# A two-block transformer on one core: another order of work in the mixing stages, and rank roots kept as four columns

## The reference

```python
# block one, mixing (8 query heads, 2 key groups, head size 64)
kc = _rope(_compress(k_cmp), ...)        # gelu(blocks @ w1) @ w2: 15 compressed keys
vc = _compress(v_cmp)
p_cmp = softmax(q @ kc)                  # compressed attention
# selected (slc), windowed (win) and sliding (swa) attention follow; then
merged = sigmoid(ga) * (o_a @ w_branch_a) + sigmoid(gb) * (o_b @ w_branch_b)
h = h + merged @ w_out

# block two, mixing
q  = rmsnorm(cq, g_q) @ w_uq             # rank 768 -> 8 heads x 96, rope on 32 of 96
kv = rmsnorm(ckv, g_kv) @ w_ukv          # rank 256 -> keys and values of 8 heads
o_a = mla_attention(...)                 # dense, 8 heads
o_b = dsa_attention(...)                 # sparse: index scores, top 64, 4 heads
o_c = silu(rg) * head_groupnorm(retention(...))
x = x + concat(o_a, o_b, o_c) @ w_out
```

## Time and profile before

| what | value |
|---|---|
| median of 3 runs | 1364.92 us (1363.53 to 1365.43) |
| profiled execution | 1365.18 us, of it 1363.3 us from the first to the last instruction |
| mean granted TensorE clock | 0.973 of 2.4 GHz |
| TensorE busy | 1316.5 us |
| VectorE busy | 823.7 us |
| ScalarE busy | 628.6 us |
| GpSimd busy | 95.3 us |

### The profile page before, as it was taken

How to read it: one execution, slowest core, us unless ns; L and a number is a source line. 1 busy time by engine, 2 the same in 40 slices (tenths; PEclk the granted TensorE clock), 3 DMA queues, 4 the chain that set the end, 5 groups by cost and what they waited for, 6 DMA issues and landing times.

```text
span 1363.3 us, 21639 instructions
## 1 busy us (share of the span) xinstructions
PE 1316.5 (97%) x8900; PEld 1196.4 (88%) x8900; DVE 823.7 (60%) x947; ACT 628.6 (46%) x838; POOL 95.3 (7%) x73
## 2 busy tenths in 40 slices
PE   6999999999989999999999999999999999999997
PEld 4999998888979999998889789999988878899996
DVE  2665547656556565555689766555557876655554
ACT  4344445466533543334743445444464344544443
POOL 0000001200000000000542100000004230000000
PEclk7999999989989999999989899999999999999999
DMA  7555556443214565556523235555644231465551
GB/s 234 187 190 186 186 165 172 141 151 94 93 63 145 179 217 185 185 185 178 166 87 127 93 93 175 189 190 186 178 155 141 84 124 57 149 212 186 187 189 54
DMA packets 173347, 209.93 MB, mean 154 GB/s; under 512 B 24168, under 2 KB 149728, under 8 KB 173152
## 3 DMA queue, kind: packets, MB, share of 16 engines
q1 hardware_dynamic: 172976, 208.78, 48.6%
q10 hardware_dynamic: 304, 0.20, 0.1%
HBM read 207.92 MB, written 1.05 MB: 153 GB/s over the span
## 4 chain that ended last, share of the span: by engine, by line
PE 87%; DVE 5%; ACT 4%; issue 2%; POOL 1%; DMA 1%; SPq 0%; ACTq 0%; DVEq 0%; POOLq 0%
PE bank L1726 69%; PE bank L2156 4%; PE bank L2018 3%; PE bank L2039 2%; ACT w_hi L920 2%; DVE w_lo L1254 2%; PE bank L1795 2%; PE bank L1961 1%; PE bank L2025 1%; PE bank L1783 1%; POOL scr L847 1%; DMA raw<-in_ffn_gate_dram 1%; PE bank L2073 1%; ACT scr L951 1%; PE bank L2012 1%
## 5 line engine op out<-in xcount | busy, mean ns | idle before, releaser
L1254 DVE TENSOR_TENSOR w_lo<-raw,w_hi 128x2048 fp32r<-128x2048 f32 (+1 forms) x198 | 449.0, 2269 | 296.6 <-ACT w_hi L920 296.0
L1726 PE MATMUL bank<-n_hi,w_hi 128*128 128x256 f32 (+2 forms) x1696 | 488.8, 288 | 13.4 <-DVE w_lo L1254 11.4
L1726 PE MATMUL bank<-n_lo,w_hi 128*128 128x256 f32 (+2 forms) x1696 | 484.4, 286 | 0.0
L1726 PE MATMUL bank<-n_hi,w_lo 128*128 128x256 f32 (+2 forms) x1696 | 484.3, 286 | 0.0
L920 ACT ACTIVATE w_hi<-raw 128x2048 fp32r<-128x2048 f32 (+1 forms) x198 | 369.5, 1872 | 236.0 <-PE bank L1726 215.7
L1726 PEld LDWEIGHTS bank<-n_hi,w_hi 128*128 128x128 f32 (+2 forms) x1696 | 328.2, 194 | 20.2 <-DVE w_lo L1254 12.2
L1726 PEld LDWEIGHTS bank<-n_lo,w_hi 128*128 128x128 f32 (+2 forms) x1696 | 328.2, 194 | 2.3 <-issue 0.5
L1726 PEld LDWEIGHTS bank<-n_hi,w_lo 128*128 128x128 f32 (+2 forms) x1696 | 328.0, 193 | 0.0
L1726 PE MATMUL bank<-w_hi,hid_hi 128*128 128x512 f32 (+1 forms) x472 | 182.8, 387 | 1.8 <-DVE hid_lo L1321 1.5
L1726 PE MATMUL bank<-w_lo,hid_hi 128*128 128x512 f32 (+1 forms) x472 | 181.6, 385 | 0.0
L1726 PE MATMUL bank<-w_hi,hid_lo 128*128 128x512 f32 (+1 forms) x472 | 181.1, 384 | 0.0
(11 more groups left out here) (250 smaller groups left out, 1554.1 us busy)
## 6 DMA issues: line engine op xcount, KB each, us to landing
raw<-in_w_ff_dram SPq DMA_DIRECT2D x64, 1024.0 KB, 5.2
raw<-in_w_in_dram SPq DMA_DIRECT2D x31, 1024.0 KB, 5.3
raw<-in_ffn_gate_dram SPq DMA_DIRECT2D x22, 1024.0 KB, 5.3
raw<-in_ffn_up_dram SPq DMA_DIRECT2D x22, 1024.0 KB, 5.4
raw<-in_ffn_down_dram SPq DMA_DIRECT2D x22, 1024.0 KB, 4.9
raw<-in_w_out_dram SPq DMA_DIRECT2D x12, 1024.0 KB, 5.0
raw<-in_w_uq_dram SPq DMA_DIRECT2D x8, 576.0 KB, 4.1
raw<-in_w_in_dram SPq DMA_DIRECT2D x12, 256.0 KB, 4.1
```

What stands on the lines that cost most here:

```text
L1254: V.tensor_tensor(w_lo[:, s % SPLIT, 0:n], raw[:, s % RING, 0:n], w_hi[:, s % SPLIT, 0:n].bitcast(f32), ALU.subtract).then_inc(lo_ready, 1)
L1726: mm = MM(out, stat(k, a), mov(k, b), start=(first and k == 0 and n == 0), stop=(last and k == K - 1 and n == 2), skip_group_check=True)
```

## The change

Three things change.

In block one the compression of the keys moves in front of the first scores and the rest of the fill list moves up by one place: the compressed scores come behind `gate 3` instead of `gate 5`, their weighted sums behind `gate 5` and `gate 6`, and `gate 7` behind the whole attention. The compressed scores become one matmul for both key groups: the rope writes the two groups to separate row halves of `kcR`, the other halves stay zero, and 4 matmuls over 128 rows and 32 columns take the place of 8 over 64 rows and 16 columns.

In block two the roots of the ranks are taken on four columns instead of a 128 x 512 tile: the sums come out of 4 matmuls of one column (`rank`, now after `proj rk`, with GpSimd's sum in a step `rsum` at the old place), the root is taken there (`rank`, `rinv`), and a step `spread` behind `proj rq` brings it to all rows, from four diagonal matrices in `diag_r`. `rtok` goes.

Also in block two, `krope` and `ukv` move into the sparse attention, the ropes `uq2` and `uq3` between its weighted sums, and `rety` into the dense attention, behind its last scores. The group norm works in `rvt` instead of `o_tmp`.

```diff
-          ("xpe", "k"), ..., ("rope", 0, "nq1"), ("rope", 0, "sq1")]
-    fill = [("cmp1", "k"), ("cmp1", "v")] + [("gate", n) for n in range(8)]
+          ("xpe", "k"), ..., ("rope", 0, "nq1"), ("rope", 0, "sq1"), ("cmp1", "k")]
+    fill = [("cmp1", "v")] + [("gate", n) for n in range(7)]
     after = {("cmp1", "v"): [("cmpt", "k")], ("gate", 0): [("cmp2", "k"), ("cmpt", "v")],
-             ("gate", 1): [("cmp2", "v"), ("rope", 0, "kc")], ("gate", 5): [("cs", 0), ("cs", 1)],
-             ("gate", 6): [("ct", 0), ("o", 0, "cmp", 0)], ("gate", 7): [("ct", 1), ("o", 0, "cmp", 1)]}
+             ("gate", 1): [("cmp2", "v"), ("rope", 0, "kc")], ("gate", 3): [("cs", 0), ("cs", 1)],
+             ("gate", 5): [("ct", 0), ("o", 0, "cmp", 0)], ("gate", 6): [("ct", 1), ("o", 0, "cmp", 1)]}
...
-    S += [("ot", "a", 0), ("ot", "a", 1), ("ot", "b", 0), ("ot", "b", 1), ("branch",)]
+    S += [("gate", 7), ("ot", "a", 0), ("ot", "a", 1), ("ot", "b", 0), ("ot", "b", 1), ("branch",)]
...
-              ("proj", l, "ckv"), ("idx", l, 0), ("proj", l, "aq"), ("idx", l, 1), ("rank", l), ("idx", l, 2),
-              ("proj", l, "rk"), ("rope", l, "aq"), ("idx", l, 3), ("idx", l, 4), ("proj", l, "rq"), ("rope", l, "rk"),
+              ("proj", l, "ckv"), ("rsum", l), ("idx", l, 0), ("proj", l, "aq"), ("idx", l, 1), ("idx", l, 2),
+              ("proj", l, "rk"), ("rank", l), ("rope", l, "aq"), ("idx", l, 3), ("rinv", l), ("idx", l, 4), ("proj", l, "rq"),
+              ("spread", l), ("rope", l, "rk"),
...
-              ("proj", l, "rg"), ("rtok", -l), ("rope", l, "kr"), ("topk", l, 1, 0, 4), ("uq", l, 0),
+              ("proj", l, "rg"), ("rope", l, "kr"), ("topk", l, 1, 0, 4), ("uq", l, 0),
...
-        S += attention(l, [("dsa", 0), ("dsa", 1)], [("retn", l), ("uq", l, 3)], {}, 1)
-        S += [("rety", l), ("rope", l, "uq2"), ("rope", l, "uq3")]
-        S += [("krope", l), ("ukv", l)]
-        S += attention(l, [("mla", 0), ("mla", 1)], [], {}, 2)
+        S += [("s", l, "dsa", 0, 0), ("s", l, "dsa", 1, 0), ("s", l, "dsa", 1, 1), ("retn", l), ("uq", l, 3), ("krope", l),
+              ("t", l, "dsa", 0, 0), ("ukv", l), ("t", l, "dsa", 1, 0), ("pv", l, "dsa", 0, 0), ("o", l, "dsa", 0),
+              ("t", l, "dsa", 1, 1), ("rope", l, "uq2"), ("pv", l, "dsa", 1, 0), ("rope", l, "uq3"), ("pv", l, "dsa", 1, 1),
+              ("o", l, "dsa", 1)]
+        dense = attention(l, [("mla", 0), ("mla", 1)], [], {}, 2)
+        late = dense.index(("t", l, "mla", 1, 1))
+        S += dense[:late] + [("rety", l)] + dense[late:]
...
# GpSimd, krope
-                    pool.wait_ge(turnc_ready, RO[(l, "uq3")] + 1)
-                    pool.wait_ge(pv_done, ON[(l, "dsa", 1)][1])
+                    pool.wait_ge(*free_count(("s", l, "dsa", 1, 1)))
...
# ScalarE
+                elif kind == "rinv":
+                    act.wait_ge(rank_inv, st[1])
+                    for i in range(2):
+                        for t in range(NT):
+                            last = nc.scalar.activation(diag_r[:, i, t, :], con("ident"), ACT.Copy, scale=rrank[:, i, t:t + 1])
+                    last.then_inc(rank_diag, 1)
+                elif kind == "spread":
                     pb = await_bank(act, st)
-                    nc.scalar.activation(rtok[:, 2, :], pb[:, 0:T:P], ACT.Copy).then_inc(freed(st), 1)
+                    nc.scalar.activation(rstd[:, 1:3, :], halves(pb[:, :]), ACT.Copy).then_inc(r_ready, 1)
...
# VectorE, rank and rinv
+                    r = rtok[:, 0:1, :].to_broadcast([P, 2, NT])
+                    V.tensor_tensor(rrank[:, :, :], pb[:, 0:4].rearrange("p (i t) -> p i t", i=2), r, ALU.mult).then_inc(freed(st), 1)
...
+                elif kind == "rinv":
                     dve.wait_ge(rank_std, st[1])
-                    link(V.reciprocal(part, part))
-                    V.tensor_tensor(part, part, r2(), ALU.mult).then_inc(r_ready, 1)
+                    link(V.reciprocal(rrank[:, :, :], rrank[:, :, :]))
+                    V.tensor_tensor(rrank[:, :, :], rrank[:, :, :], rtok[:, 0:1, :].to_broadcast([P, 2, NT]), ALU.mult).then_inc(rank_inv, 1)
...
# TensorE, cs
-                    for h in range(8):
-                        if h == 4:
-                            settle(mm)
-                        r = slice(64 * (h // 4), 64 * (h // 4) + 64)
-                        mm = MM(pb[:, h * CP:h * CP + CP], nqT[r, h % 4, t * P:t * P + P], kcR[r, h // 4, :], start=False, stop=True,
-                                skip_group_check=True)
+                    by_group = pb[:, 0:P].rearrange("p (g r c) -> p r g c", g=2, r=4)
+                    for r in range(4):
+                        mm = MM(by_group[:, r], nqT[:, r, t * P:t * P + P], kcR[:, :, :], start=False, stop=True, skip_group_check=True)
...
# TensorE, rank and spread
-                    MM(pb[:, 0:T], ones[:, :], sq[:, 0, :], start=True, stop=True)
-                    MM(pb[:, T:2 * T], ones[:, :], sq[:, 6, :], start=True, stop=True).then_inc(filled(st), 1)
+                    for i in range(2):
+                        for t in range(NT):
+                            mm = MM(pb[:, 2 * i + t:2 * i + t + 1], sq[:, 6 * i, t * P:t * P + P], ones[:, 0:1], start=True, stop=True)
+                    mm.then_inc(filled(st), 1)
+                elif kind == "spread":
+                    pb = take(pe, st)
+                    pe.wait_ge(rank_diag, st[1])
+                    for i in range(2):
+                        for t in range(NT):
+                            c = (2 * i + t) * P
+                            mm = MM(pb[:, c:c + P], ones[:, :], diag_r[:, i, t, :], start=True, stop=True)
+                    mm.then_inc(filled(st), 1)
```

More of the change, by code:

```diff
@@ L381, in job @@
         def job(key, b=None, freed_by=None, of_slab=False):
-            if b is None and idle[0] and key[0] in ("rope", "rtok", "toks", "idx", "rank"):
+            if b is None and idle[0] and key[0] in ("rope", "toks", "idx", "rank", "spread"):
                 b = _small[0] % 4
@@ L879, in _ @@
                     add_up([(slice(0, 3), slice(3, 6)), (0, 1), (0, 2), (6, 7)])
+                if st[0] == "spread":
                     pool.wait_ge(r_ready, RN[st] + 1)
@@ L1499, in _ @@
                     ahead(SL[st])
+                    dve.wait_ge(r_ready, RN[("spread", st[1])] + 1)
                     for n in range(4):
@@ L1519, in _ @@
                     dve.wait_ge(turnc_ready, r + 1)
-                    V.tensor_tensor(dst, view[2], view[0], ALU.add).then_inc(rope_done, 1)
+                    if st[2] == "kc":
+                        for g in range(2):
+                            rows_ = slice(64 * g, 64 * g + 64)
+                            last = V.tensor_tensor(dst[rows_, g], view[2][rows_, g], view[0][rows_, g], ALU.add)
+                        last.then_inc(rope_done, 1)
+                    else:
+                        V.tensor_tensor(dst, view[2], view[0], ALU.add).then_inc(rope_done, 1)
                     turn_used[0] = (rope_done, r + 1)
@@ L1872, in _ @@
                         mm = nc.tensor.transpose(pb[:, t * w_:t * w_ + w_], by_feature[0:w_, t * P:t * P + P], ident[0:w_, 0:w_])
-                    mm.then_inc(filled(st), 1)
-                elif kind == "rtok":
-                    pe.wait_ge(r_ready, RN[("rank", -st[1])] + 1)
-                    pb = take(pe, st)
-                    for t in range(NT):
-                        mm = nc.tensor.transpose(pb[:, t * P:t * P + P], rstd[:, 2, t * P:t * P + P], ident)
                     mm.then_inc(filled(st), 1)
```

33 lines of the change are left out of this document (16 added, 17 removed).

## The result

| what | before | changed |
|---|---|---|
| median | 1365.18 us (1363.53 to 1365.64, 4 runs) | 1349.84 us (1347.48 to 1354.16, 4 runs) |
| profiled execution, its span | 1365.18, 1363.3 us | 1347.48, 1345.7 us |
| mean granted clock in it | 0.973 | 0.989 |

The ratio is 0.990, 95% interval 0.9879 to 0.9922: 15.3 us less at the median, 17.6 us between the two profiled spans. The four executions of the changed kernel lie further apart than those of before (6.7 us against 2.1), and the profiled one is their fastest, so what follows accounts for the 17.6 us and not for the 15.3. The forecast was 1346.0 us, in 1336 to 1356.

The account below looks back on a forecast made before the run. TensorE, busy 97% of the span, was taken as the bound; 5.4 + 8.0 + 0.9 + 2 x (4.3 + 3.5 - 2.0) = 25.9 us, less 6.8 for clock falls, gave 19.1: 1365.1 to 1346.0 us, range 1336 to 1356.

Parts of the forecast that it names:

- Part 1 and 2: Block one: compression ahead of first scores, net 5.4 us despite a new 2.1 us wait; joined compressed scores, 8.0 us.
- Part 3: Tail of block one's attention: 1.51 us wait goes, 1.93 us wait grows by 0.6; gain 0.9 us.
- Part 4: Rank roots, both layers: the wait for GpSimd's sum and its half clock go; net gain 4.3 us each.
- rival (c): Rank change trades its wait for one behind GpSimd; ending slower than before, 1365 us and up; chance 0.03.
- Part 5: Key-value slab inside the sparse attention, both layers: 6.1 us go, new waits come; net gain 3.5 us each.
- three blocked splits: Key-value slab: GpSimd's copy and both rope products each block a split, some 2 us worse per layer.
- Part 6: Group norm's end inside the dense attention, both layers: four VectorE instructions delay a copy; loss 2.0 us each.
- Four places: Block one's first weighted sum, both dense attentions, compressed scores: clock falls, even chances, 3.4 us each; -6.8 us for two.
- rival (b): Whole kernel: new waits are longer and the clock falls at all four places, 1352 to 1357 us; chance 0.23.
- (a): Whole kernel: the clock never falls again, gain 26 us or a little more, 1333 to 1339 us; chance 0.17.
- Rival (d): Whole kernel: half-clock stretches return as long as before, only waits move; gain about 0 to 6 us; chance 0.07.

Follow-up runs that it names:

- the second profile: The changed kernel run once more, unchanged, beside the kernel before: 1350.22 us (1348.07 to 1351.09), ratio 0.9892.

## Why the prediction was right, and where a step of it was wrong

The sum was 25.9 us without falls, 19.1 with two of four; 17.6 us came in the profiled execution and 15.3 at the median. The terms were further off than their sum: the key-value part gave 2.2 us less than forecast (both layers) and block one 1.2 less, while the rank roots gave 0.9 more and the clock cost 5.6 us in place of 6.8. That these nearly cancel is luck.

- **Part 1 and 2, block one.** Right in mechanism. The wait at the first scores went, and one came ahead of the first weighted sum, 0.79 + 1.01 us (forecast 2.1 in one piece). This is the step where the splits queue:

```profile
285.11 4.49 DVE L1267 TENSOR_TENSOR w_lo<-raw,w_hi 128x2048 fp32r<-128x2048 f32 x2 [4.21 <-ACT w_hi L929]
289.52 0.68 DVE L1582 COPY probsT<-bank 128x512 f32<-128x512 f32 x1
```

  The splits end at 289.6 and the copy stands behind them, forecast 289.4 and 290.0. The clock fell there (3.4 us). The compressed scores take 0.93 us each, from first record to first record (2.27 before, forecast 1.1), and stayed at full clock, in this profile and in the eight others that have them:

```profile
336.58 0.23 PE L2058 MATMUL bank<-masks,identb 128*128 128x128 bf16 x1
336.64 1.03 PE L2061 MATMUL bank<-kcR,scr 128*128 128x32 f32 x8
337.51 0.22 PE L2058 MATMUL bank<-masks,identb 128*128 128x128 bf16 x1
```

- **Missed in block one: 1.3 us.** The weighted sums of the compressed attention wait 1.28 and 1.87 us, 3.2 in all (L2072 in the list of waits), where the kernel before waited 0.96 twice, 1.9. The forecast has no term for them; that the faster TensorE reaches them sooner is likely, and no run tests it.
- **Part 3.** The 1.5 us wait went. The wait for the last split grew from 1.9 to 2.9 us, forecast 2.5.
- Together parts 1 to 3 gave 9.7 us; with the fall of 3.4 put back that is 13.1, forecast 14.3. The missed waits are about the difference.
- **Part 4.** 4.55 and 4.53 us, and 0.2 a layer for the two transposes that went further down: 4.75, forecast 4.3. The records of the rank sums span 0.95 us and stand 0.11 us apart, TensorE's only wait on GpSimd is one of 2.1 us that both kernels have, and its waits for weights (11.3 us in the longest group, 11.4 before) did not grow: rival (c) is out.

```profile
690.66 0.95 PE L2090 MATMUL bank<-ones,scr 128*128 128x1 f32 x8
```

- **Part 5 was mis-sized:** 2.5 and 2.3 us, forecast 3.5. Its largest term, 3.4 us for the slow clock behind the sparse attention, is the one that failed: with the gap filled in the kernel before, that fall was worth 0.9 us in layer 1, since VectorE sets the pace of the slab. The terms against it were wrong for the same reason. The slab waits 0.75 and 1.59 us (forecast 1.4 and, for the product beside the copy, 0.5), but at 11.89 us it is as long as the 11.84 of the kernel before with filled gaps, which waits 0.31 and 1.83 us: most of this was there already, under the slow clock. So the real sum is 0.9 for the clock, 2.6 for the two waits gone (2.35 and 0.28), less 0.2 for waits in the slab beyond those 2.14, less 0.66 at the dense scores (forecast 0.7): 2.6 us. The 2 us a layer that three blocked splits would have cost did not come: the copy met a product (1.37 us lost), the first rope product no split, and the second one split that lost 0.47 us. Here is TensorE:

```profile
750.76 0.39 PE L1745 MATMUL bank<-hid_hi,w_hi 128*128 128x256 f32 x1 [0.75 <-DVE probsT L1582]
...
754.04 0.50 PE L1745 MATMUL bank<-w_hi,hid_hi 128*128 128x512 f32 x1 [1.59 <-DVE scr L1516]
...
762.89 0.39 PE L2024 MATMUL bank<-masks,identb 128*128 128x512 bf16 x1 [0.66 <-DVE scr L1540]
```

- **Part 6.** 2.06 us lost in each layer, forecast 2.0: four instructions of VectorE from 773.60 to 775.96 and then the copy; the weighted sum waits for it:

```profile
776.62 1.10 PE L2051 MATMUL bank<-scr,probsT 128*128 128x64 f32 x8 [1.95 <-DVE probsT L1582]
```

- **The clock.** Four places were given even chances. In the profiled execution it fell at one (part 1), and a fifth place, layer 2's first projection, cost 1.6 us. That is one of the prediction's own signs of being wrong, that the clock falls in other places than the four; but the change did not make this one, for the wait ahead of it is in both kernels, and the kernel before with filled gaps has the fall there too (1006.4). In the second profile it fell at three of the four (both dense waits too), at the compressed scores in neither. Over all profiles even chances fit the dense waits, behind which it fell eight times of twelve, but not the other two: at part 1's pair of waits, 0.8 and 1.0 us, it fell in all six profiles that have the pair, at the new compressed scores in none of nine. Two of the eight executions of the changed kernel, 1352.0 and 1354.2 us, lie in rival (b)'s range, and none in (a)'s. Rival (d) is out: of the six long stretches one is left in the first profile and three are there in the second, and 15 us were gained.

What stays open: why the clock falls behind one and the same gap in one execution and not in the next, why never behind another of the same length, and where it fell in the slower executions of the kernel with only the gate splits mended.

## What to carry to other kernels

Where TensorE is the bound, count a wait on it with what the clock adds behind it, but credit that surcharge only if the next engine is ready earlier too: look at the first wait behind the slow stretch. When steps are moved in a list that fixes every engine's queue, look for the splits and evacuations that now stand ahead of a small copy; moving three of these by a step or so gave 13 us more here, nearly as much again as the change itself. A profile is one execution: two of the same kernel had their slow stretches in different places, so read waits from it, and what the clock costs from several.

## What the runs showed of the hardware

How often the granted clock fell to half behind a gap of TensorE, over the thirteen profiles. A fall is counted where half clock begins between the start of the gap and 2.7 us behind its end.

| gap, us | where | falls |
|---|---|---|
| 2.9 | first projection of layer 1, for a weight split | 11 of 13 |
| 2.9 | ahead of the branch products, changed block one | 4 of 8 |
| 2.4 | first scores of block one, as before | 4 of 4 |
| 2.35 | weighted sum of the sparse attention, as before | 6 of 6 |
| 1.95 | dense attention, group norm in one piece | 8 of 12 |
| 1.93 | ahead of the branch products, as before | 0 of 4 |
| 1.9 | second compressed weighted sum, changed | 1 of 9 |
| 1.85 | first projection of layer 2, for a weight split | 5 of 13 |
| 1.56 | rank sums, as before | 6 of 6 |
| 1.6 | inside the moved key-value slab | 0 of 12 |
| 0.8, then 1.0 | first transposes and weighted sum, changed block one | 6 of 6 |
| 0.8 | bank of gate 0, gate splits one by one | 1 of 3 |
| filled | with matmuls of zeros | 0 of 5 |

- A half-clock stretch of 6.83 us beside a busy VectorE cost 0.9 us, one of the same length at the rank sums 3.0.
- The 8 records of the rank sums, one column each, stand 0.11 us apart, those of the 256-column projections 0.12: with 128 x 128 new weights each time, one column is hardly cheaper than 256.
- A VectorE instruction with two SBUF operands that started beside a running GpSimd instruction took longer by what was left of that one, less 0.14 us: 1.37, 1.09 and 0.47 us for 1.51, 1.23 and 0.61 left.
